# Back pass of the recurrence and gated products joined in one block: outputs by token rows, last tokens first, loads in one queue

## What is computed

```python
o_f, s_f = hgrn_direction(q, v, f_fwd, ..., s0_fwd)             # gated linear recurrence, first token to last
o_b, s_b = hgrn_direction(q[::-1], v[::-1], f_bwd[::-1], ...)   # the same, last token to first
o = o_f + o_b[::-1]                                             # 4 heads of 128
o = o * rsqrt(mean(square(o), axis=-1) + RMS_EPS) * norm_g      # per token and head
o_hgrn = o * silu(og)
y = sigmoid(g_four) * (fourier_mix(u) @ w_fp) + sigmoid(g_hgrn) * (o_hgrn @ w_hp)
```

## Time and profile before

| | us |
|---|---|
| median of three runs | 3351.34 |
| the profiled execution, own time | 3350.46 |
| its span (first to last instruction) | 3348.6 |
| TensorE busy | 3115.2 (93%) |
| VectorE busy | 1851.5 (55%) |
| ScalarE busy | 615.8 (18%) |
| POOL busy | 302.3 (9%) |
| granted TensorE clock, mean | 0.971 |

### The profile page before, as it was taken

One profiled execution on the slowest core, in us unless ns is written; L12 is line 12 of the kernel. 1 busy time (PEld: TensorE's weight loads), 2 busy tenths in 40 slices (PEclk: granted clock), 3 DMA queues, 4 the chain that ended last, 5 costly groups with the idle time before them and its releaser, 6 DMA issues. The chain is left out here.

```text
span 3348.6 us, 35637 instructions
## 1 busy us (share of the span) xinstructions
PE 3115.2 (93%) x14552; PEld 2555.9 (76%) x14552; DVE 1851.5 (55%) x2585; ACT 615.8 (18%) x1048; POOL 302.3 (9%) x453
## 2 busy tenths in 40 slices
PE   6999999999996899739969999999999999999997
PEld 3888888888883788627758878888888788888886
DVE  5821132122215888458667766666656656666556
ACT  2421000111113566420002221111111111111110
POOL 0322110100002212200000000000000000000000
PEclk9999999999998999969989999999999999999999
DMA  6732233333326433355545521211115222211111
GB/s 224 256 97 86 78 115 103 110 123 123 118 80 212 123 101 119 109 182 169 177 162 187 175 84 57 63 61 54 54 51 155 95 67 63 69 52 53 51 45 63
DMA packets 261127, 365.32 MB, mean 109 GB/s; under 512 B 15443, under 2 KB 171363, under 8 KB 259430
## 3 DMA queue, kind: packets, MB, share of 16 engines
q1 hardware_dynamic: 203926, 197.33, 19.4%
q0 software_dynamic: 43680, 134.26, 11.6%
q10 hardware_dynamic: 13360, 31.46, 2.9%
HBM read 256.55 MB, written 106.44 MB: 108 GB/s over the span
## 5 line engine op out<-in xcount | busy, mean ns | idle before, releaser
L1985 PE MATMUL tail_bank<-tail_h2h,tail_w1h 128*128 128x512 f32 x1024 | 400.1, 391 | 4.5 <-DVE tail_w1l L1754 4.5
L144 PE MATMUL head_bank<-head_hTh,head_wh 128*128 128x512 f32 x1024 | 401.1, 392 | 3.1 <-DVE head_hTl L561 2.3
L2003 PE MATMUL tail_bank<-tail_w2h,tail_ah 128*128 128x512 f32 x1024 | 399.6, 390 | 4.0 <-DVE tail_acc L1784 4.0
L1986 PE MATMUL tail_bank<-tail_h2l,tail_w1h 128*128 128x512 f32 x1024 | 399.7, 390 | 0.0
L1987 PE MATMUL tail_bank<-tail_h2h,tail_w1l 128*128 128x512 f32 x1024 | 399.5, 390 | 0.0
L2004 PE MATMUL tail_bank<-tail_w2l,tail_ah 128*128 128x512 f32 x1024 | 399.5, 390 | 0.0
L2005 PE MATMUL tail_bank<-tail_w2h,tail_al 128*128 128x512 f32 x1024 | 399.4, 390 | 0.0
L146 PE MATMUL head_bank<-head_hTh,head_wl 128*128 128x512 f32 x1024 | 398.7, 389 | 0.0
L145 PE MATMUL head_bank<-head_hTl,head_wh 128*128 128x512 f32 x1024 | 398.6, 389 | 0.0
L569 DVE CAST head_wh<-head_raw 128x1024 fp32r<-128x1024 f32 x64 | 44.6, 698 | 546.9 <-PE head_bank L146 414.7
L1786 DVE TENSOR_TENSOR tail_acc<-tail_acc,tail_bank 128x512 f32<-128x512 f32 x416 | 275.4, 684 | 118.7 <-PE tail_bank L2005 116.5
(11 more groups left out here) (228 smaller groups left out, 4745.4 us busy)
## 6 DMA issues: line engine op xcount, KB each, us to landing
tail_raw<-in_w SPq DMA_DIRECT2D x128, 512.0 KB, 4.0
head_raw<-in_w_in SPq DMA_DIRECT2D x64, 512.0 KB, 4.1
scratch_proj<-head_stage POOLq DMA_DIRECT2D x128, 256.0 KB, 2.7
head_x<-in_w_ada ACTq DMA_DIRECT2D x8, 2048.0 KB, 10.2
merge_gates<-scratch_proj SPq DMA_DIRECT2D x32, 512.0 KB, 5.5
head_wa<-in_w_ada SPq DMA_DIRECT2D x8, 1024.0 KB, 9.3
mix_dec<-scratch_proj SPq DMA_DIRECT2D x32, 256.0 KB, 4.2
scratch_dft_a<-mix_fa POOLq DMA_DIRECT2D x32, 256.0 KB, 4.2
```

What stands on the lines that cost most here:

```text
L144: nc.tensor.matmul(out, wh, xh, start=(k == 0), stop=False)
L1985: nc.tensor.matmul(U[2 * e + c][:], w1h[:, e, k, :], hT[0][:, k, cs], start=(k == 0), stop=False)
L1986: nc.tensor.matmul(U[2 * e + c][:], w1h[:, e, k, :], hT[1][:, k, cs], start=False, stop=False)
L2003: nc.tensor.matmul(V[n % 4][:], ah[:, z, ts], w2h[:, z, cs], start=(first and z == strips[0]), stop=False)
```

## The change

`phase_merge` goes; its work is put into `phase_mix`.

- Fourier: all 48 pieces of kind b now run in steps 4 to 17 (three a step in steps 4 to 11, four in steps 12 to 17). `load_x` moves to the top of the following step in POOL's list. The last channel group of the Fourier result stays in SBUF.
- What the back pass needs (`qd`, `ub`) is stored to DRAM by POOL in every step and loaded again by SP; ScalarE's `keep` goes.
- Both outputs are formed with tokens on partitions: the operands of the matmuls change places. The forward output is stored once (256 KB a chunk); the backward one stays in PSUM and VectorE adds the forward one to it.
- The norm is taken per token: ScalarE squares with a running sum into a 128x4 tile and takes the root of that, VectorE the reciprocal of the 128x4 tile. TensorE then turns the chunk back to channels x tokens.
- The first four back steps run ahead of the strips. The other twelve are spread over the strips of the first three token blocks, at fixed places `BACK` and `TURN`, in TensorE's list in front of the strip's products.
- Strips (a tile m of a block) go through the token blocks last to first. Gates have three buffers, and y is formed in the gates' own buffer. So a load of gates now waits for the *store* of the tile three before.
- All loads stand in one list of SP.

The core of the diff (new lines of the strips and of what feeds them; the loop's bookkeeping is left out):

```diff
+        later = [("b", j, piece) for j in range(16) for piece in range(3)]
+            lo = 3 * (p - 4) if p < 12 else 24 + 4 * (p - 12)
+            return later[lo:lo + (3 if p < 12 else 4)]
+        BACK, TURN = (0, 1, 3, 5), (1, 3, 5, 6)
...
+            def load_gates(n):
+                bi, m = divmod(n, KD)
+                if n >= 3:
+                    sp.wait_ge(st_y[n % 3], 16 * (n // 3))
...
+                sp.dma_start(gates[:, n % 3], src[m][:, :, c0:c0 + 512]).then_inc(ld_g[n % 3], 16)
+            def load_back(x):
+                c = NC - 1 - x
...
+                sp.dma_start(qd[:, x % 2], d["qd"][c]).then_inc(ld_qd[x % 2], 16)
...
+                sp.dma_start(of[:, x % 2], d["o"][c * P:(c + 1) * P, :]).then_inc(ld_of[x % 2], 16)
...
+            for bi in range(NB):
+                x0 = 4 * (bi + 1)
+                for m in range(KD):
+                    n = bi * KD + m
+                    if n + 3 < NB * KD:
+                        load_gates(n + 3)
+                    if bi == NB - 1:
+                        continue
+                    if m in (0, 1, 3):
+                        load_four(bi + 1, min(m, 2))
+                    if m in (2, 4, 6, 7):
+                        x = x0 + {2: 2, 4: 3, 6: 4, 7: 5}[m]
+                        if x < NC:
+                            load_back(x)
+                        if x + 1 < NC:
+                            load_kept(x + 1)
```

The strips of VectorE, of ScalarE (two lines, same loops) and of TensorE (same loops), in this order; ahead of them the same pieces for x = 0 to 3, with `low_weights(4)` to `(7)` between them and, in SP's list, `load_w(6)` in front of `load_back(2)` and `load_w(7)` in front of `load_back(3)`:

```diff
+            for bi in range(NB):
+                x0 = 4 * (bi + 1)
+                for m in range(KD):
+                    if bi < NB - 1:
+                        if m in TURN:
+                            output_gate(x0 + TURN.index(m))
+                        if m in BACK:
+                            both_ways(x0 + BACK.index(m))
+                        if m in TURN:
+                            low_o(x0 + TURN.index(m))
+                        if m in BACK:
+                            step_back(x0 + BACK.index(m) + 1)
+                            normalise(x0 + BACK.index(m))
+                        if m in (2, 4):
+                            low_four(bi + 1, m - 2)
+                            low_four(bi + 1, m - 1)
+                    gated(bi * KD + m)
...
+                    if m in (1, 3):
+                        round_four(bi + 1, m - 1)
+                        round_four(bi + 1, m)
...
+                    if bi < NB - 1:
+                        if m in TURN:
+                            turn_back(x0 + TURN.index(m))
+                        if m in BACK:
+                            back_output(x0 + BACK.index(m))
+                    if bi or m >= 3:
+                        from_fourier(bi, m)
+                    from_states(bi, m)
```

More of the change, by code:

```diff
@@ L713, in phase_mix @@
[L713 to L722 removed]
+        bx.line("mix")
+        base = -(-nc.sbuf_base // 32) * 32
+        K = 1024
@@ L732, in phase_mix @@
         st_f = bx.sem("st_f")
-        step_s, kk, ksum, q_in, masked, wide_s, big_s, qd_s = (bx.sem(x) for x in (
-            "step", "keys", "key_sum", "queries", "masked", "wide", "big", "queries_kept"))
+        step_s, kk, ksum, q_in, masked, wide_s, big_s = (bx.sem(x) for x in (
+            "step", "keys", "key_sum", "queries", "masked", "wide", "big"))
         tot_s, upd_s, kx_s, sc_s = ([bx.sem(f"{x}{s}") for s in range(2)] for x in ("totals", "climbed", "sides", "scores"))
@@ L848, in _ @@
                     load_q(c + 2)
+                if c == 0:
+                    sp.dma_start(ng[:], d["norm_g_col"]).then_inc(ld_m, 16)
+                if c in (2, 4, 6):
+                    load_w(c - 2)
+                    load_w(c - 1)
+            for n in range(3):
+                load_gates(n)
+            load_four(0, 0)
+            load_four(0, 1)
+            load_back(0)
+            load_kept(1)
+            load_four(0, 2)
+            load_back(1)
+            load_kept(2)
+            load_w(6)
+            load_back(2)
+            load_kept(3)
+            load_w(7)
+            load_back(3)
+            load_kept(4)
+            load_back(4)
+            load_kept(5)
+            load_back(5)
+            load_kept(6)
+            for bi in range(NB):
[14 more added lines that the diff above has]
+                            load_kept(x + 1)
         @block.vector
@@ new lines, in gated @@
+            def gated(n):
+                dve.wait_ge(ld_g[n % 3], 16 * (n // 3 + 1))
+                dve.wait_ge(mm_s, n + 1)
+                pb, gt = pair[n % 3], gates[:, n % 3]
+                step.up(nc.vector.tensor_tensor(gt[:, 0, :], gt[:, 0, :], pb[0][:], ALU.mult))
+                step.up(nc.vector.tensor_tensor(gt[:, 1, :], gt[:, 1, :], pb[1][:], ALU.mult))
+                step.wait(dve)
+                nc.vector.tensor_tensor(gt[:, 1, :], gt[:, 0, :], gt[:, 1, :], ALU.add).then_inc(y_s, 1)
@@ L1292, in _ @@
                 c = p
+                if p == 4:
+                    load_x(0)
+                    load_x(1)
+                if p > 4:
+                    for _, j, piece in parts_at(p - 1):
+                        if piece == 1 and j + 2 < 16:
+                            load_x(j + 2)
                 if c + 1 < NC:
@@ new lines, in _ @@
+                if p > NX:
+                    store_u(p)
+                if 0 < p <= NC:
+                    store_q(p - 1)
+                if p >= 4:
+                    for _, j, piece in parts_at(p):
+                        if piece == 2 and j % 4 == 3 and j < 15:
+                            store_four(j // 4)
+            store(NC - 1)
+            for n in range(NB * KD):
+                bi, m = divmod(n, KD)
+                c0 = (NB - 1 - bi) * 512
+                pool.wait_ge(y_s, n + 1)
+                pool.dma_start(d["y"][m * P:(m + 1) * P, c0:c0 + 512], gates[:, n % 3, 1, :]).then_inc(st_y[n % 3], 16)
@@ L1535, in phase_tail @@
+            for s in range(3):
+                pool.wait_ge(st_y[s], 16 * len(range(s, NB * KD, 3)))
 def phase_tail(nc, d, g):
```

526 lines of the change are left out of this document (267 added, 259 removed).

## The result

The changed kernel takes **3435.7 us** in the median of four runs (3432.28 to 3438.67), the kernel before 3350.43 (four runs, 3348.52 to 3353.53): a ratio of 1.0253 with a 95% interval of 1.0236 to 1.0271, 85 us slower. 3425 us was forecast, 3370 to 3480 the range. The profiled execution took 3436.26 us, its span 3434.5.

A forecast was written before the change was run, and what follows sets the result against it. It took TensorE and VectorE to hold each other in the loop and TensorE to bound the strips. From 3350.5 us, -46 for the strips' earlier start, -15 for their work and +136 for waits gave 3425 us, range 3370 to 3480.

The forecast's parts named there:

- SP's list, and the links: Strips: loads queue behind y's store landing; a link, from gated's end to a small load landed, 8.7 us; waits 119.5 us.
- The estimate by the Trainium skill: Strips: a transfer taken as about 2.0 us plus bytes over 436 GB/s; link 7.2 us, result 3404 us.
- The clock, and the strips' own work: Strips: 188 us of TensorE work without waits, against 203 before; lower clock after waits adds 16 us.
- From T to the strips: Lead-in from the last forward output to the states' first product: 51 us, bounds T+45 and T+62; start at 1440.
- T: The end of the loop's last forward output, 1378.8 us before the change, forecast 10 us later.
- The loop: Recurrence loop: +10 us, 8 from extra Fourier pieces and 2 from `low_weights`.
- nothing for these three: Loop: POOL's added stores, SP's weight-load waits and ScalarE's lost copies were taken to cost no time.
- Rival C: Loop: POOL's two stores wait for late events, 2.5 us in 14 steps, +35, giving 3460 us; chance 5%.
- Rival A: SP's list in the strips: loads are in time, the 136 us are not paid, giving 3290 us; chance 7%.
- break-even of 3.4: Strips: us a link at which waits and clock cost 61 us, cancelling the savings; best store and load 5.2 already.
- Rival B: Heads of strips 3 and 5: one link instead of two, waits 4.9 us each, giving 3338 us; chance 5%.
- The terms of a turn: Lead-in: one back step's load issues and landing, `back_output` and VectorE's six operations, 11.7 us a turn, two turns.

The follow-up runs named there:

- experiment 1: Changed kernel with only SP's list in the strips reordered, all loads issued ahead of the late store wait: 3304.51 us.
- experiment 2: Changed kernel with only the Fourier loads moved ahead in SP's list, the back pass's loads left: 3402.77 us.
- experiment 8: Changed kernel with all loads ahead, y in its own buffers, loop weights one step later, and load_w(6), load_w(7) behind load_back(2), load_back(3): 3280.39 us.
- experiment 7: Changed kernel with load_w(6) and load_w(7) put behind load_back(2) and load_back(3) ahead of the strips: 3422.09 us.
- experiment 9: As experiment 8, but the loop's weights load behind steps 4, 6 and 8, two steps later than in the changed kernel: 3278.07 us.
- experiment 4: Changed kernel with three separate buffers for y, so gates' loads wait for the gated tile and not its store: 3403.46 us.

## Why the prediction was right

By its own steps:

- **SP's list, and the links.** Shown. The waits stand where they were placed, 124.4 us against 119.5, and experiment 1 takes them away by the order of SP's list alone. A link measured 8.1 and 9.2 us in one pair; 8.7 was taken, from the rows of the same transfers in the old strips. Its parts were off in opposite ways: the store landed after 2.4 us where 3 was taken, and the small load was there 5.5 and 6.5 us after the issue of the gates' load, where 5.3 was. That the low part of a Fourier tile stands ahead of the next `gated` in VectorE's list, which makes the chain one of two links, is shown by experiment 2, where the wait falls from 17 to 11 or 12 us.
- **The estimate by the Trainium skill** ("DMA: Bandwidth & Descriptors", Anatomy of one DMA — SWDGE (gpsimd) path), 7.2 us a link and 3404 in all, came out low. The page gives its fit for the DMAs that GpSimd issues. The stores of y are of this kind, and the trace agrees: 2.4 us to landing in both links, where the fit makes it 2.6 for 256 KB. The gates' load goes by SP's queue; the prediction put it by the same fit at 3.2 us, and it took 5.3 in the median of the run after.
- **The clock, and the strips' own work.** Strips without their waits: 328.7 - 124.4 = 204.3 us, against 188 + 16 = 204. That this agrees to 0.3 us is partly luck. In experiment 8 TensorE is busy 184.95 us with the same 876 matmuls, at 0.99 of the clock, and 204.15 us here, at 0.79: the work is 3 us less than the 188, and the lower clock costs 19.2 us and not 16.
- **From T to the strips.** 49.6 us, 51 forecast. The first Fourier product comes at T+12.8 (T+13). They start at 1441.94 us, 1440 forecast, since the loop's end is 7.3 us later than taken, the loop began 3.8 us earlier and the stretch is 1.4 us shorter. SP's order is part of the stretch (`load_back(2)` behind `load_w(6)`): 13 us by experiment 7.
- **The loop: +17.3, +10 forecast.** This step was wrong in one term. The extra Fourier pieces cost some 4.9 us (steps 12 and later and the way to T) where 8 was taken, `low_weights` 2.1 (steps 5 and 7) where 2 was, and the first three steps are 1.0 us longer. But the prediction had "nothing for these three", SP among them: it asked whether SP's weight loads wait, not who waits for what is behind them. 1 MB stands ahead of a Fourier load that is due at once, in the step where the transform's first half ends; the later pairs of weights cost nothing of the kind. Steps 3 and 4 pay 9.3 us; with the weights two steps later (experiment 9) they take 17.8 and 27.3 us, 0.9 more than before in all, while the total of that experiment can't be told from its neighbour's. Rival C, a loop that pays 35 us by POOL's stores, did not occur; steps 8 to 11 take 18.9 us.
- **Rival A** (loads in time, 3290 us) is what experiment 1 makes: 3304.5 us. Most of the 14.5 us between them are the 7 us of the loop and two waits left in the strips, 4.6 and 1.7 us. Its ground for a low chance (the order, not the bandwidth) holds. The 5.2 us that it calls store and load at their best adds a best store to a median load; its break-even of 3.4 stays below either way.
- **Rival B** (one link) had a wrong price: 3338 us was worked out with a strip too many taken off. With 10.3 us for 4.9 in six waits, and the 8 us of clock that it had left out, its sum is 3378, and experiment 2, which is that case, gives 3403. Of the 25 between them 7 are the loop's and 17 are longer waits: 89.5 us in all against 72.6 by the mended sum, the two at strip 0 among them with 7.7 and 7.8. The case is 1.4% slower than the kernel before, not faster. So the 11% for a faster result, which counted most of B, was too high; the forecast doesn't hang on it.
- **Small readings.** The "106 us of slack" ahead of the strips is the length of the stretch; TensorE was busy for 44 of it, so 62 were idle. The terms of a turn, given as 11.7, add up to 11.6.
- **Not in the forecast**: the 3.8 us ahead of the loop, 2.1 in the block change and 2.5 in the tail. The first and the last are within what runs of the same code differ by: over the changed kernels step 0 starts at 1047.2 to 1053.9 us (1051.0 before), and the tail takes 1636.1 to 1639.6 (1637.1 before). The wait at the block change is 24.2 to 24.5 us in the changed kernels against 22.2; its cause stays open.

The forecast of 3425 was 11 us low: 5 in the waits, 7 in the loop, and small terms that nearly cancel. The mechanism was right; that single terms such as the clock and the strips' work came out so near is in part errors that cancel.

## What to carry to other kernels

In a list that an engine works through in order, a wait holds not its own instruction but everything written behind it: put each load where its buffer becomes free, ahead of any wait on the product of this very round, and ask of every entry who waits for the next one. A bulk load without a due time (weights) belongs behind the small ones that are due. When waits come by two ways (here Fourier loads and back-pass loads), mend both before judging either, since each alone gave 33 and 75 of 131 us.

## What the runs showed that was not expected

- TensorE's waits for the load of `mix_qd` were shown as "issue", 136.8 us in 11 waits, and never under the name of the load, so a reader has to look at SP's list to find the cause.
- To take the store of y (2.3 us at best) out of the chain gave 2.3 us a link and not more, though the 0.3 us to its issue by POOL go as well. In experiment 4 the loads start while the store still moves, and both land later: the store after 5.8 us in the median where it took 2.4, `mix_qd` after 6.5 where it took 6.0.
- `back_output`'s eight matmuls took 2.05 us behind each long wait, where they took 1.13 behind the short one of 1.23 us (1.13 before too): the whole group runs at the lower clock, and the waits cost TensorE its clock on top, 19 us in all.
